# The order of the query blocks of a head pair in the prompt attention of a two-layer decoder step: one head after the other, or the two heads in turn

## What is computed

```python
# A: scores of each query block against its causal keys, bias by distance, softmax, values
s = jnp.einsum('btngd,btknd->btkng', qg, kg).reshape(bx, t, k, h).astype(jnp.float32) + bias
s = jnp.where(valid[..., None], s, -jnp.inf)
p = jnp.exp(s - lse[:, :, None, :])
o = jnp.einsum('btkng,btknd->btngd', p.astype(vg.dtype), vg)
# C: the same over the topk keys of each query
_, idx = lax.top_k(score, topk)
o, _ = gathered_attention(q_blk, take_rows(k, idx), take_rows(v, idx),
                          rel_bias_for(rel_bias, dist, h), dist >= 0)
```

## Time and profile before

| what | value |
|---|---|
| median of three runs | 1622.85 us (1618.48 to 1628.53) |
| profiled execution, its own time | 1623.6 us |
| its span, first to last instruction | 1621.4 us |
| TensorE busy | 1545.2 us, 95% of the span |
| VectorE, ScalarE, GpSimd busy | 676.1, 656.1, 684.4 us |
| chain of work that ended last | 86% TensorE; L652 68%, L740 3%, L719 3%, L728 2% |
| mean granted clock of TensorE | 0.963 of full speed |

### The profile page before, as it was taken

The page is one execution under the profiler, slowest core; times in us unless marked ns, Lnnn a source line. Parts: engine busy times, 40 slices in busy tenths (PEclk is TensorE's granted clock), DMA queues, the critical chain, the costliest instruction groups (busy, mean ns, idle before and its releaser), DMA issues.

```text
span 1621.4 us, 31069 instructions
## 1 busy us (share of the span) xinstructions
PE 1545.2 (95%) x12246; PEld 1486.5 (92%) x12246; DVE 676.1 (42%) x1181; ACT 656.1 (40%) x1083; POOL 684.4 (42%) x350
## 2 busy tenths in 40 slices
PE   7999988699999999999989996999999999999998
PEld 7999887499999999999979775999999999999998
DVE  4154355215443434322350568765544444431224
ACT  5233465204334444222363554664334444332234
POOL 4644561014444444444435456220434444444444
PEclk9999879769999999999999997999999999999999
DMA  4222332112222222333224322122222222233323
GB/s 171 94 92 64 124 121 71 59 63 91 88 91 93 91 91 91 91 104 103 82 66 126 108 79 66 54 58 62 91 78 91 91 91 91 91 91 103 102 93 118
DMA packets 52835, 146.88 MB, mean 91 GB/s; under 512 B 5485, under 2 KB 18057, under 8 KB 52250
## 3 DMA queue, kind: packets, MB, share of 16 engines
q1 hardware_dynamic: 50866, 138.22, 27.0%
q10 hardware_dynamic: 1896, 7.67, 1.3%
HBM read 139.11 MB, written 6.76 MB: 90 GB/s over the span
## 4 chain that ended last, share of the span: by engine, by line
PE 86%; DVE 7%; ACT 3%; issue 1%; SPq 1%; DMA 1%; POOL 0%; ACTq 0%; DVEq 0%
PE PS L652 68%; PE PS L740 3%; PE PS L719 3%; PE PS L1020 2%; PE PS L728 2%; PE PS L998 1%; DVE act_lo L1596 1%; PE PS L668 1%; PE PS L717 1%; DVE top L1939 1%; SPq L330 1%; DMA w_raw<-in_w 1%; PE PS L1053 1%; PE PS L1108 1%; ACT w_hi L1193 0%
## 5 line engine op out<-in xcount | busy, mean ns | idle before, releaser
L487 POOL TENSOR_TENSOR w_lo<-w_raw,w_hi 128x1024 fp32r<-128x1024 f32 x217 | 535.1, 2466 | 853.6 <-ACT w_hi L1193 853.6
L652 PE MATMUL PS<-act_hi,w_hi 128*128 128x260 f32 x2592 | 743.7, 287 | 24.4 <-DVE act_lo L1596 11.2
L652 PE MATMUL PS<-act_lo,w_hi 128*128 128x260 f32 x2592 | 735.5, 284 | 0.0
L652 PE MATMUL PS<-act_hi,w_lo 128*128 128x260 f32 x2592 | 734.8, 284 | 0.0
L652 PEld LDWEIGHTS PS<-act_hi,w_hi 128*128 128x128 f32 x2592 | 491.5, 190 | 40.1 <-issue 27.5
L1193 ACT ACTIVATE w_hi<-w_raw 128x1024 fp32r<-128x1024 f32 x217 | 230.0, 1060 | 724.9 <-PE PS L652 715.5
L652 PEld LDWEIGHTS PS<-act_lo,w_hi 128*128 128x128 f32 x2592 | 492.0, 190 | 0.4
L652 PEld LDWEIGHTS PS<-act_hi,w_lo 128*128 128x128 f32 x2592 | 492.0, 190 | 0.0
L652 PE MATMUL PS<-h_hi,w_lo 128*128 128x260 f32 x704 | 198.8, 282 | 0.0
L652 PE MATMUL PS<-h_hi,w_hi 128*128 128x260 f32 x704 | 198.6, 282 | 0.0
L652 PE MATMUL PS<-h_lo,w_hi 128*128 128x260 f32 x704 | 198.5, 282 | 0.0
(11 more groups left out here) (322 smaller groups left out, 1807.3 us busy)
## 6 DMA issues: line engine op xcount, KB each, us to landing
w_raw<-in_w SPq DMA_DIRECT2D x217, 512.0 KB, 3.5
kcA<-in_cache_k SPq DMA_DIRECT2D x8, 512.0 KB, 4.6
vcA<-in_cache_v SPq DMA_DIRECT2D x6, 512.0 KB, 5.1
biasC<-scratch_rows SPq DMA_DIRECT2D x12, 256.0 KB
x<-in_xT SPq DMA_DIRECT2D x4, 520.0 KB, 6.2
out_y<-x SPq DMA_DIRECT2D x8, 260.0 KB, 4.4
biasA<-scratch_rows SPq DMA_DIRECT2D x8, 256.0 KB
kcC<-in_pool_k SPq DMA_DIRECT2D x16, 128.0 KB, 2.5
```

The costliest lines, as they stand in the source:

```text
L487: pool.tensor_tensor(w_lo[:, s, :], w_raw[:, s, :], w_hi[:, s, :].bitcast(F32), ALU.subtract).then_inc(S("w_lo"), 1)
L652: mm = pe.matmul(PS[:, 2 * place + half, 0:HALF], w[:, s, j * P:(j + 1) * P], r[:, c, cols], start=first and n == 0 and i == 0, stop=last ...
```

## The change

The eight units of a pair come in another order: `(par, qb)` = (0,3) (1,0) (0,2) (1,1) (0,1) (1,2) (0,0) (1,3), so the widths are 512, 128, 384, 256, 256, 384, 128, 512, and the heads alternate. Three kinds of conditions follow it. The waits for the end of a head's four units (`par + 9` instead of `4 * par + 6`) now name the seventh unit for `par` 0 and, as before, the eighth for `par` 1; they stand on SyncE for the bias rows of A and of C, and on GpSimd for the values of A. The waits at the start of a pair (`staged`, `t_o`) and of a head (`bias`) go by the first units in the new order. And `start` of the output products, which was tied to the unit alone, is tied to its first key block too.

```diff
         def units_of(pairs):
-            return [(p, par, qb) for p in range(pairs) for par in range(2) for qb in range(QB)]
+            return [(p, par, qb) for p in range(pairs) for par, qb in TURNS]
+
+        TURNS = ((0, 3), (1, 0), (0, 2), (1, 1), (0, 1), (1, 2), (0, 0), (1, 3))
+        FIRST = TURNS[0:2]
...
             def biases_a(pairs):
...
                         if p >= 2:
-                            sp.wait_ge(S("t_x"), BASE_A + 8 * (p - 2) + 4 * par + 6)
+                            sp.wait_ge(S("t_x"), BASE_A + 8 * (p - 2) + par + 9)
                         head_bias(sp, p, par, biasA, 2 * p + par)
...
             def biases_c(pairs):
...
-                        sp.wait_ge(S("t_x"), BASE_C + 8 * (p - 2) + 4 * par + 6)
+                        sp.wait_ge(S("t_x"), BASE_C + 8 * (p - 2) + par + 9)
                         head_bias(sp, p, par, biasC, head_c(p, par))
...
                     if pair >= 2:
-                        pool.wait_ge(S("t_v"), 8 * (pair - 2) + 4 * par + 6)
+                        pool.wait_ge(S("t_v"), 8 * (pair - 2) + par + 9)
                     pool.tensor_copy(vA[par][:, pl, :, own[par]], vtokA[:, :, c:c + HD]).then_inc(S("A_st"), 1)
...
                 def scores(i):
                     p, par, qb = units[i]
-                    if par == 0 and qb == 0:
+                    if (par, qb) == TURNS[0]:
                         staged(p)
...
                 def out(i):
                     p, par, qb = units[i]
-                    if par == 0 and qb == 0:
+                    if (par, qb) == TURNS[0]:
                         pe.wait_ge(S("t_o"), base // 8 + p + 1)
...
-                                       pt[:, i % 2, kb * P:(kb + 1) * P], start=i % 8 == 0,
+                                       pt[:, i % 2, kb * P:(kb + 1) * P], start=i % 8 == 0 and kb == 0,
                                        stop=i % 8 == 7 and kb == qb)
...
             def bias_a(i, unit, W):
                 p, par, qb = unit
-                if qb == 0:
+                if (par, qb) in FIRST:
                     dve.wait_ge(S(f"bias{p % 2}{par}"), p // 2 * 16 + 16)
...
             def bias_c(i, unit, W):
                 p, par, qb = unit
-                if qb == 0:
+                if (par, qb) in FIRST:
                     dve.wait_ge(S(f"bias{p % 2}{par}"), 16 * (p // 2) + 48)
```

## The result

The changed kernel takes 1625.61 us (median of 20 runs, 1623.22 to 1628.29), the kernel before 1621.65 us in 20 runs of the same comparison (1616.91 to 1628.53). The ratio is 1.0022 with a 95% interval of 1.0012 to 1.0033: 3.6 us slower, between 1.9 and 5.3. The forecast (1624, no change to speak of) holds, but the loss is larger than its 0.9.

The account below looks back on a forecast made before the run. TensorE, already streaming, was taken to bound both attentions. From the profiled 1623.6 us, fill +0.4, staging +0.5 and the rest 0 gave 1624.5, or 1623.7 seen from the median; forecast 1624, range 1618 to 1632.

Parts of the forecast that it names:

- likeliest case: Whole kernel: no change to speak of, time within 3 us, chance 0.80.
- fill: Start of layer 0's attention: third scores wait 0.26 us for the wide unit's addition, taken as +0.4; layer 1 zero.
- staging: GpSimd splitting later queries and keys beside VectorE's scalings: +0.5 us at two layer 0 places; layer 1 0, within 1.5.
- copy gap: ScalarE's copy between transpositions and output products: fits everywhere, once by 0.02; cost 0, or 0.8 us if 0.1 late.
- drain: End of an attention: wide unit last in both orders, so same but for short work ahead; 0, within 0.3 us.
- TensorE as the bound: Both attentions: TensorE streams, a layer 0 pair stays 10.44 us in any order, more even steps gain nothing.
- worst case: Layer 0 beside GpSimd's splitting: narrow and wide scalings both stretched, transpositions 0.7 us late at worst, 0.6 taken.
- own sign of being wrong: TensorE waiting on ScalarE's copy in every pair would show that the gap of 0.75 us was too small.
- Today's waits: Rival: 0.36 us waits beside GpSimd's splitting vanish at eight places, -2.9 us, 1621; chance 0.06.
- GpSimd meets the wide scaling each time: Rival: each of eight splittings costs TensorE 1.0 us instead of 0.36, +5 to +7, up to 1631; chance 0.10.
- The clock was not lost: Rival: small waits in every step drop TensorE's granted clock to 0.50, 16 us or more, 1640 up; chance 0.04.
- Queues: Moved requests for bias rows and value copies on SyncE and GpSimd: still in time, cost zero.

Follow-up runs that it names:

- e11: Changed kernel with the new order only in the first pair of either layer, the old order in the other ten pairs; ratio to before 0.9991 (0.9970 to 1.0013).
- e5: Changed kernel put back to the old order, GpSimd subtracting only 8 of 512 columns from the third pair on; layer 0's attention 45.59 us, layer 1's 115.12.
- e6: Changed kernel, new order kept, GpSimd subtracting only 8 of 512 columns from the third pair on; layer 0's attention 47.26 us, layer 1's 117.80.
- e9: Changed kernel with the old order in the last pair of either layer; ratio to before 1.0011 (1.0000 to 1.0022).
- e10: Changed kernel's order a second time from the experiments' kernel text, nothing else changed; layer 0's attention 48.80 us, layer 1's 119.18.
- e2: Changed kernel with the same order of widths but heads not alternating; ratio to before 1.0010 (0.9995 to 1.0024).

## Why the prediction was right, and where its sum was not

The forecast was no change to speak of, and the time lies in its range, within 1% of before. The range is wide because the runs scatter, and it would have held twice the loss; that it holds the time says little for the sum. The likeliest case, within 3 us, was narrowly missed: 3.1 by the stages, 3.6 (1.9 to 5.3) by the runs. The sum said +0.9; at the same rise of the clock the terms now are:

| term | forecast | A | C | shown by |
|---|---|---|---|---|
| fill | +0.4 | +0.5 | +0.2 | first pairs, e11 |
| staging | +0.5 | +0.7 | +0.3 | e5, e6 |
| copy gap | 0 (0.8 if it fails) | +0.3 | 0 | seventh step 1.29 |
| drain | 0, within 0.3 | +0.6 | +0.5 | last pairs, e9 |
| sum | +0.9 | +2.1 | +1.0 | |

The sum is 3.1, as the stages say, beside the 3.6 (1.9 to 5.3) measured. A later rise of the clock, which is in no term, comes on top in some executions; the two profiled ones do not show it.

**TensorE as the bound.** Right. With the staging thinned out a pair of the old order takes the 10.44 to the hundredth (e5), and one of the new order, with the same eight widths, 10.53 and 10.52 (e6), which is 10.44 and the late copy. Evenness bought nothing.

**The fill.** The mechanism and the size of its wait were right (0.36 for 0.26, taken as 0.4). One thing was left out: a pair that begins a stage lacks the transpositions of three earlier units, 1.01 us of them in the old order (widths 2, 3, 4), 0.88 in the new one (3, 1, 4), so 0.13 more are left in the first pair. Together that is 0.49, beside the 0.46 between e11 and before, whose clock rose at the same time. The 0.23 to 0.26 that the wide unit's products wait for their copy in after and e10 are not there in e11, where the clock rose 0.7 to 0.8 later; they take the place of time at half clock. In C no wait shows in the fill, as forecast.

**Staging.** The prediction's worst case came: both scalings stretched, 0.77 lost where 0.6 was taken, so +0.36 instead of +0.24 at each of the two places, 0.7 for 0.5. In C the six places were put at zero within 1.5, and the six pairs are at 0, +0.36, +0.20, -0.24, +0.02 and -0.01: 0.3 in all, inside the bounds. The stretch itself stays under the Trainium skill's rule that was weighed ("SBUF — State Buffer", "Who interferes with whom"), taken with the scaling's whole time behind GpSimd's: the narrow scaling would take the 1.21 left of GpSimd's instruction and its own 0.29, 1.50, and the wide one 1.11 and 0.49, 1.60; the rows say 1.29 and 1.39. Both are 0.21 less, and so is the row that the prediction kept, by 0.20 (1.41 for 1.61). So the rows agree with the wait that the rule states if 0.2 of the scaling's own time passes during it.

**The copy gap.** The prediction's own sign of being wrong came, late copies in every pair of A, though without idle time in the profile. The step that failed is "It holds everywhere, once by only 0.02". The time at which the copy ends was right; that TensorE needs it a tenth earlier, for the weight load, was missing. With 0.10 more in the bill, 0.83 for three blocks and 0.94 for four, exactly one of the gaps named there (0.75) is too short and the others (0.85, 1.02, 1.36) are not, which is what the steps show. The fallback of 0.1 at two places was at one, and not in C.

**The drain.** The largest miss, 1.1 of the 2.2 that the sum lacked: "The last unit is the wide one in both orders, so the drain is the same but for the order of the short work ahead of it". It is the same chain, but that order of the work ahead changed it in two ways, and not within 0.3. The sixth unit, now three blocks wide instead of two, has a longer copy and longer products ahead of the last transpositions and delays them by 0.33; its place behind the last exponential, which the expectation of e9 names, is the same in both orders. And the last step but the drain holds less: the eighth scores are followed by t2 and o2 (0.61) instead of t1 and o4 (0.92), so 0.31 us of TensorE's work moved from behind the last scores, where TensorE has idle time anyway, to ahead of them, where everything waits for it. Together that is 0.64 in A. The prediction walked through the fill row by row, but not through the drain.

**The rivals.** Today's waits did not vanish; in A they grew. GpSimd meets the wide scaling each time in A, at 0.77 and not 1.0, but in C only in the third pair (0.79), which is why the 5 to 7 us did not come. The clock was not lost in the middle of either stage: 1.00, with TensorE idle 1.08 of 18 us in A; so the rival that the Trainium skill's "TensorE: Matmul & The Clock Gate", "A second HAM failure mode: psum-queue depth-cycling", stands behind does not apply at one or two waits of half a microsecond in a pair.

**Queues.** Zero, as forecast: no wait for a bias shows, and e2, with other release points, has the same pairs.

## What to carry to other kernels

Reordering equal work behind a bound that already streams can only move the ends and the collisions: cost the first and the last round of a pipeline as carefully as the middle, counting what work lies behind the last start of the longest chain. When a gap is checked for a hand-over, take the time at which the consumer first touches the data (here the weight load, 0.10 us ahead of the product), and include what stands ahead of the producer in its own queue. For effects of 2 or 3 us in 1600 read stage lengths in the traces, and compare only stages whose clock fell and rose at the same times.

## What the runs showed of the hardware

A TensorE group that has to wait for its weights' data costs about 0.1 us more than the wait that the profile shows: 0.68 instead of 0.59 with no idle time in the row at all.

The granted clock rose 3.3 to 8.2 us after the first scores of A and 4.9 to 9.2 after those of C, in kernels whose work up to there was the same or differed in the order only, and in C each microsecond of it was worth half a microsecond of time. Where the clock had fallen 14.7 to 15.0 us ahead of the first scores of C, the rises in the two orders lay more than 3 us apart (5.6 to 5.8 and 8.9 to 9.2).

A VectorE scaling that started just behind a GpSimd subtraction ended behind it by its own undisturbed time less 0.2: 0.08 for 128 columns (0.29 undisturbed), 0.22 for 384 (0.42), 0.28 for 512 (0.49). So beside a subtraction of 1.3 us a scaling of 128 columns took 1.29 and one of 512 only a tenth more, 1.39.
